# The second input projection as seven half-block products in place of eight, with weight sums formed in the first

## The chip, the cores and the metric

One NeuronCore of a Trainium2 chip runs the whole program. The metric is the device time of one execution in microseconds.

## The reference

Two decoder layers run for a prompt of 2048 tokens and for 64 sample tokens (8 sequences of 8), with D_MODEL = 1024. Layer 0 runs gated linear attention and retention side by side; layer 1 is a gated DeltaNet with a causal convolution of width 4. Each layer is

```
x <- x + gate(c) * RMSNorm_post(mixer(RMSNorm_pre(x) * (1 + scale(c)) + shift(c)))
```

What the change touches is layer 1's input projection and what follows it directly: the normed and scaled tokens h (2048 + 64 by 1024) times a weight array of 1024 by 4112. Its first 3072 columns are q, k and v, which then pass the convolution over tokens and a silu; the next 1024 are the gate z, which passes a silu; the last 16 are the write strength and decay. All inputs are float32, and results are compared with a float32 reference, so each product is formed in three passes (below).

## The kernel before, in words

The phases run one after the other: `inab` (`phase_in_ab`, L630, the first input projection, to about 603 us), `mixab` (`phase_mix_ab`, L1352, the first mixer, to about 1011), `inc` (`phase_in_c`, L1882, the second input projection, 1012.8 to 1746.7) and `mixc` (`phase_mix_c`, L2355, the second mixer).

Both projections are tiled alike. Tokens go in four blocks of 512. A group is one PSUM bank of 128x512: `product` (L620, its matmul is L625) runs over 8 k tiles of 128 and over PASSES, which are high x high, high x low and low x high, since every operand is kept as a 16-bit upper half and a 16-bit lower half. That makes 24 matmuls of 512 columns a group. PE works through the groups of a block in an order written out by hand, and ACT evacuates each bank; four banks form a ring.

`inab` has 27 groups a block. Blocks 1 and 2 run from 167 to 311 and from 311 to 455 us. ACT evacuates gate and value groups at L913 into `inab_vz`, from where SP stores them (L800); POOL forms lower halves (`split_lo`, L537) and the norm's rstd (L403, L405); DVE rotates q and k (L1030 to L1037, "r chain"), which SP stores at L784. `Prep` (L337) prepares the next block's four tiles of 128 tokens: a square sum on ACT, rstd on POOL, the norm on DVE (L410), eight transposes on PE (L417, "tile turn"), scaling on ACT and DVE (L498, L508), upper halves on ACT and lower halves on POOL. SP's waits, stores and loads stand in one fixed order for each block.

`mixab` ends with `Early` (L1258), which prepares the first 512 tokens of layer 1 beside the last of the mixer: scaling, upper and lower halves (L1319 on ACT, L1336 on DVE, L1342 on POOL). Then `Finish` (L1133) closes the sample tokens: DVE's copy L1732, two small matmuls, a pow on POOL, two DVE operations, a store (L1202). SP also loads the first weights of layer 1.

`inc` keeps all of its weights in SBUF: in block 0, ACT (L568) and POOL (L574) split them into halves while PE works. A block is 24 qkv groups, 8 z groups, one quarter group (the last 16 columns, four column strips of PE at once) and one group that turns its result. ACT moves a qkv group to `ub` (L2071), DVE runs the convolution on it (L2169 to L2175: halo copy, one multiply, three multiply-adds), ACT applies silu (L2064), SP stores it. After the last block the sample tokens follow: their own products (L2314), turns, the decay chain on ACT, and a sample convolution on DVE (L2208 to L2215). The last DMAs of the phase are issued at L2152 and L2153, and `mixc` begins with L3088.

Of the kernel before, what the change touches and what calls it, by code (L numbers as in the profile page):

```python
# [206 lines left out]
def phase_ada(nc, io, modT):  # L207

    io["modT"] = modT
    io["cT"] = nc.dram_tensor("tmp_cT", (P, KT * C9), F32, kind="Internal").ap()  # L210

# [407 lines left out]

def product(nc, dst, lhs, rhs, before=lambda k: None):  # L620
# [9 lines left out]
def phase_in_ab(nc, io, modT, seq):  # L630
# [67 lines left out]

    c_in, silu, ctr, cT_ready = ph.sem("c_in"), ph.sem("silu"), ph.sem("ctr"), ph.sem("cT_ready")
# [22 lines left out]
    unit_at = {g: [AHEAD + i for i, s in enumerate(slots) if s == g] for g in slots}  # L722

# [9 lines left out]
    def _(sp):  # L733
# [26 lines left out]

        def outputs(b, n, tiles, next_loads):
# [9 lines left out]
            next_x(0)  # L771
            sp.wait_ge(u_done, b + 1)
# [9 lines left out]
            next_x(1)  # L782
            sp.wait_ge(r_done, b + 1)
# [12 lines left out]
            for j in range(4 * tiles):  # L796
# [4 lines left out]
                             vz[:, j % 4, :]).then_inc(vz_out[j % 4], 16)  # L801
                if j == 4:
                    next_x(3)
# [5 lines left out]
        with sp.Fori(0, nb - 2) as b:  # L809
            outputs(b, BLK, TPB, [(4 * b + 6 + tc, tc % 2, P) for tc in range(4)])  # L810
            rot_load(b + 1, BLK)
        b = nb - 2
        outputs(b, BLK, TPB, [(4 * b + 6 + tc, tc % 2, (P, P, NS, 0)[tc]) for tc in range(4)])
        rot_load(b + 1, BLK)
# [10 lines left out]
        sp.wait_ge(pre_in, 64)  # L825
        for i in range(4):
            sp.wait_ge(vz_out[i], 16 + 16 * nt + (32 if i < 2 else 0))
# [3 lines left out]
    def _(pool):  # L831
# [30 lines left out]
    def _(act):  # L862
# [27 lines left out]
        def groups(b, n, next_square, first=False, rows_at={}):  # L890
            chain.turn(2 * b)

            for q, g in enumerate(order(n)):
# [50 lines left out]
                if first and g in GATES:  # L944
                    cond.gates(act, GATES[g])
                if g in rows_at:
# [7 lines left out]
        for b in range(1, nb - 1):  # L954
            groups(b, BLK, [(4 * b + 4 + tc, P) for tc in range(4)])
        rows_out.load(act, 0)
# [4 lines left out]
    def _(dve):  # L961
# [20 lines left out]

        def work(b, n, next_tiles):
# [13 lines left out]

            nx(0)

# [13 lines left out]
            nx(1)  # L1013
            dve.wait_ge(decays, b + 1)
# [13 lines left out]
            nx(2)  # L1028
            dve.wait_ge(cs_in, 16 * (b + 1))
# [2372 lines left out]
```

## Time and profile before

| | |
|---|---|
| runs | 2570.91 us median of 3 (2569.47 to 2582.24) |
| profiled execution | 2569.45 us, its span 2567.6 us |
| PE busy | 2422.2 us, 94% of the span |
| DVE, ACT, POOL busy | 1259.1, 862.2, 780.3 us |
| first input projection | to 603 us, four blocks of 144 us |
| second input projection | 1012.8 to 1746.7 us |

PE is TensorE's matmuls, PEld its weight loads (they run beside matmuls), DVE is VectorE, ACT ScalarE, POOL GpSimd, SP the engine that issues most DMAs. Busy time says how long an engine had work; whether it sets the time is read from the windows and from what ended its idle times.

### The profile page before, as it was taken

The numbers are of one execution on the slowest core, as the hardware profiler recorded it, in microseconds if no ns is written. First come the engines' busy times: TensorE is split into PE (matmuls) and PEld (weight loads), VectorE is DVE, ScalarE is ACT, GpSimd is POOL, SyncE is SP. The second block draws the span as 40 slices with busy tenths as digits, with TensorE's granted clock in tenths as the row PEclk, the third lists the DMA queues.
The fourth block names the chain that finished last, engine by engine and source line by source line (L and its number), as shares of the span: only waits on it lengthen the run. The fifth ranks groups of instructions, "written<-read, shape, count | busy, mean of one in ns | idle before, by whom it ended". The sixth has DMA issues, their size and how long they took to land. (4 is left out here: it accounts for less than half of the span.)

```text
span 2567.6 us, 52403 instructions
## 1 busy us (share of the span) xinstructions
PE 2422.2 (94%) x20691; PEld 1467.2 (57%) x20756; DVE 1259.1 (49%) x2613; ACT 862.2 (34%) x2490; POOL 780.3 (30%) x847
## 2 busy tenths in 40 slices
PE   6989999997899987999999999996899999999997
PEld 2444444444556632444444444455788888888885
DVE  3431213131687753993543626515546464554655
ACT  2633232222111113442322322225444444545431
POOL 2540000021111102551010000005656566565653
PEclk8999999998999997999999999998999999999998
DMA  8541202134544544552121112116523132222213
GB/s 297 154 146 42 99 33 91 38 119 152 203 141 155 176 165 122 155 163 84 66 71 54 62 55 80 50 43 172 141 72 105 60 106 70 84 92 81 79 32 94
DMA packets 254515, 270.00 MB, mean 105 GB/s; under 512 B 30263, under 2 KB 188023, under 8 KB 254314
## 3 DMA queue, kind: packets, MB, share of 16 engines
q1 hardware_dynamic: 186762, 219.27, 26.0%
q10 hardware_dynamic: 67552, 47.84, 6.6%
q8 instruction: 152, 2.49, 0.4%
q14 instruction: 49, 0.40, 0.0%
HBM read 179.70 MB, written 87.36 MB: 104 GB/s over the span
## 5 line engine op out<-in xcount | busy, mean ns | idle before, releaser
L625 PE MATMUL inc_b<-raw_next,inc_w_hi 128*128 128x512 f16 (+1 forms) x760 | 227.9, 381 | 3.2 <-POOL inc_w_lo L574 2.0
L625 PE MATMUL inc_b<-keep,inc_w_hi 128*128 128x512 bf16 (+1 forms) x762 | 227.2, 379 | 1.4 <-ACT inc_ub L2071 0.2
L625 PE MATMUL inab_b<-inab_wt,keep 128*128 128x512 f16 x768 | 168.3, 381 | 10.2 <-POOL inab_wt L574 10.2
L625 PE MATMUL inab_b<-inab_wt,raw_next 128*128 128x512 f16 x768 | 166.4, 379 | 0.0
L1171 PE MATMUL mixab_y<-keep,mixab_oT_hi 128*128 128x512 f16 x512 | 152.5, 379 | 7.6 <-DVE mixab_f_y L1251 5.9
L2173 DVE SCALAR_TENSOR_TENSOR inc_acc<-inc_ub,inc_taps,inc_acc 128x512 f32<-128x512 f32 x192 | 152.0, 792 | 6.8
L2071 ACT ACTIVATE inc_ub<-inc_b 128x512 f32<-128x512 f32 x96 | 56.9, 593 | 251.1 <-PE inc_b L625 247.0
L625 PE MATMUL inc_b<-raw_next,inc_w_lo 128*128 128x512 bf16 x368 | 140.1, 381 | 0.0
L625 PE MATMUL inc_b<-keep,inc_w_lo 128*128 128x512 bf16 x366 | 138.8, 379 | 0.0
L2169 DVE COPY inc_ub<-inc_halo 128x3 f32<-128x3 f32 x96 | 26.0, 271 | 228.3 <-ACT inc_ub L2071 228.3
L625 PEld LDWEIGHTS inab_b<-inab_wt,keep 128*128 128x128 bf16 (+1 forms) x768 | 75.2, 98 | 101.0 <-issue 12.7
L625 PEld LDWEIGHTS inc_b<-raw_next,inc_w_hi 128*128 128x128 f16 x768 | 75.3, 98 | 91.3 <-issue 3.0
L625 PEld LDWEIGHTS inab_b<-inab_wt,raw_next 128*128 128x128 bf16 (+1 forms) x768 | 75.1, 98 | 90.0
L625 PEld LDWEIGHTS inc_b<-keep,inc_w_hi 128*128 128x128 f16 x768 | 75.0, 98 | 89.4
L913 ACT ACTIVATE inab_vz<-inab_b 128x512 f32<-128x512 f32 x66 | 39.2, 598 | 243.6 <-PE inab_b L625 181.3
L2576 POOL TENSOR_TENSOR mixc_levels<-mixc_BT,raw_next 128x512 f32<-128x512 f32 (+1 forms) x82 | 110.2, 1374 | 1.5 <-DVE mixc_BT L2862 1.5
L410 DVE TENSOR_SCALAR keep<-keep,inab_rstd 128x1024 f32<-128x1024 f32 (+1 forms) x13 | 10.2, 788 | 204.6 <-POOL inab_rstd L405 204.4
L1171 PE MATMUL mixc_y<-mixc_w_hi,mixc_oT_hi 128*128 128x512 f16 x256 | 98.1, 383 | 6.7 <-DVE mixc_oT_lo L2954 6.7
L537 POOL TENSOR_TENSOR raw_next<-keep,raw_next 128x1024 f16<-128x1024 f32 x12 | 27.6, 2296 | 249.7 <-ACT raw_next L532 249.7
L537 POOL TENSOR_TENSOR keep<-keep 128x1024 f16<-128x1024 f32 x12 | 26.4, 2202 | 243.4 <-ACT keep L532 243.4
L1171 PE MATMUL mixc_y<-mixc_w_hi,mixc_oT_lo 128*128 128x512 f16 x256 | 97.6, 381 | 0.0
L1171 PE MATMUL mixc_y<-mixc_w_lo,mixc_oT_hi 128*128 128x512 f16 x256 | 97.6, 381 | 0.0
(590 smaller groups left out, 5954.5 us busy)
## 6 DMA issues: line engine op xcount, KB each, us to landing
tmp_qkv<-stage_next SPq DMA_DIRECT2D x98, 256.0 KB, 2.0
stage_next<-in_w_in_c ACTq DMA_DIRECT2D x30, 512.0 KB, 4.5
inab_stage<-in_w_in_ab ACTq DMA_DIRECT2D x24, 512.0 KB, 4.1
raw_next<-tmp_qkv SPq DMA_DIRECT2D x8, 1536.0 KB, 6.7
mixc_qkv<-tmp_qkv SPq DMA_DIRECT2D x8, 1536.0 KB
inab_wt<-in_w_ada SPq DMA_DIRECT2D x10, 1024.0 KB, 15.3
keep<-in_x_prompt SPq DMA_DIRECT2D x16, 512.0 KB, 4.1
tmp_v<-inab_vz SPq DMA_DIRECT2D x32, 256.0 KB, 4.0
```

What stands on the lines that cost most here:

```text
L410: dve.tensor_scalar(self.xn[0:n, :], self.x[par][0:n, :], self.rs[0:n, par:par + 1], None, ALU.mult).then_inc(self.xnd, 1)
L537: pool.tensor_tensor(room[1][:, :, col:col + n], self.hf[:, :, 0:n], room[0][:, :, col:col + n], ALU.subtract).then_inc(self.lo_done, 1)
L625: last = nc.tensor.matmul(dst, lhs(a, k), rhs(b, k), start=(k == 0 and i == 0), stop=(k == KT - 1 and i == len(PASSES) - 1))
L913: act.activation(vz[:, j % 4, :], src[:], ACT.Copy if j < (2 * TPB if n == BLK else 1) else ACT.Silu).then_inc(evac, 1)
L1171: last = self.nc.tensor.matmul(self.banks[half][0:n, :], (self.oT_hi, self.oT_lo)[a][:, h, 0:n], self.w[b][:, h, half * 512:(half + 1) * 512],
L2071: act.activation(ub[g % 2][:, CONV - 1:], src[:], ACT.Copy).then_inc(evac, 1)
L2169: chain.link(dve.tensor_copy(u_[:, 0:CONV - 1], h_))
L2173: chain.link(dve.scalar_tensor_tensor(a_v, win(i), taps[:, c, i:i + 1], a_v, ALU.mult, ALU.add))
L2576: pool.tensor_tensor(BTm[w][0:n], BT[0:n, :, 0:HB], bc(tv[f"pick{w}"][0:n].unsqueeze(1), [n, H, HB]), ALU.mult).then_inc(btm_ready, 1)
```

## The change

**Seven products for eight.** A step of `inc` is now a 2x2 block product: two channel tiles of 128 by the block's two halves of 256 tokens, with k in two halves of 512. In Winograd's form, seven products of sums of quarters replace eight, each of 4 k tiles x 3 passes = 12 matmuls of 256 columns. There are 64 steps, 16 a block: 12 "units" for q, k and v (channel tiles u and u + 4) and 4 z steps, "gate items", one after every three units. In the last block a unit step has 288 columns: 32 of the sample tokens ride along with each half. The order on PE is `begin(n)` (products 1 and 6), `finish(n-1)` (4 and 3), `rest(n)` (2, 5 and 7). Between them ACT forms the first sum and the c11 corner, DVE the second and third sum and the corners c22, c21 and c12 from PSUM; the corners go to `ub`. The convolution's first multiply is now ACT's, its halo copies are POOL's, and a `Pairs` class replaces `Prep`: it forms differences of the tokens' quarters on DVE, upper halves on ACT and lower halves on POOL (3 parts a set, 6 sets of 3584 elements a partition, one small sample set).

**Weight sums.** The seven weight factors (four of them the sums s1 to s4, three plain quarters) of all 16 unit columns are formed in blocks 1 and 2 of `inab` by `PairWeights`, in 64 steps, 32 a block. A step: SP loads four 128x128 quarters, DVE forms the sums into a spare PSUM bank, ACT the upper halves, POOL and DVE the lower halves, SP stores both to DRAM (`tmp_w7`). There is one buffer `a_out` for the plain quarters, and two of everything else. In `inc` they are streamed: a ring of two slots of 1.8 MB each (one unit's seven factors, 7 DMAs of 256 KB with rows of 2 KB), refilled by SP as soon as a product has used its factor. The z factors (4 x 1.8 MB) are loaded at the start of `inc`, ahead of the refills. The SP and DVE loops of `inab` are written out; POOL's work there stands by group.

**The end of `mixab`.** `Early` also forms differences and the 7 operands of block 0, and SP loads the ring's two slots (14 DMAs) before it stores the sample tokens.

**The sample work of `inc`** moves between the last block's steps: halo and strengths after step 3 and 4, cumulated sums after 5, turned tails and sample convolutions after 8 and 12, the sample's z product after 10; only the last third of tails and sample convolution is left for the end.

```diff
+class PairWeights:
...
+    def next(self, sp, n):
+        u, k = divmod(n, 4)
+        sp.wait_ge(self.a_lo, n + 1)
+        sp.dma_start(self.dst[u, 0:3, :, k].rearrange("m p e x -> p m e x"), self.a_out[:]).then_inc(self.a_stored, 16)
+        if n + 2 < PAIR_STEPS:
+            sp.wait_ge(self.s_done, n + 1)
+            self.load(sp, n + 2)
+        if n >= 1:
+            self.store_s(sp, n - 1)
...
+        dve.tensor_tensor(s1, a21, a22, ALU.add).then_inc(self.s1_done, 1)
+        dve.tensor_tensor(s3, a11, a21, ALU.subtract)
+        dve.wait_ge(self.s1_done, n + 1)
+        dve.tensor_tensor(s2, s1, a11, ALU.subtract).then_inc(self.s2_done, 1)
+        dve.wait_ge(self.s2_done, n + 1)
+        dve.tensor_tensor(s4, a12, s2, ALU.subtract).then_inc(self.s_done, 1)
...
+    def hi(self, act, n):
+        act.wait_ge(self.raw_in[n % 2], 32 * (n // 2 + 1))
+        wait(act, self.a_stored, 16 * n)
+        act.activation(self.a_out[:, :, 0, :], self.raw[n % 2][:, P:4 * P].rearrange("p (m x) -> p m x", m=3), ACT.Copy).then_inc(self.a_hi, 1)
+        act.wait_ge(self.s_done, n + 1)
+        wait(act, self.s_stored[n % 2], 16 * (n // 2))
+        act.activation(self.s_out[n % 2][:, :, 0, :], self.banks[n % 2][:].rearrange("p (m x) -> p m x", m=4), ACT.Copy).then_inc(self.s_hi, 1)
...
+        pool.tensor_tensor(self.a_out[:, :, 1, :], self.raw[n % 2][:, P:4 * P].rearrange("p (m x) -> p m x", m=3), self.a_out[:, :, 0, :],
+                           ALU.subtract).then_inc(self.a_lo, 1)
...
+    W7_TWICE = (16, 18, 20, 22, 24, 26, 28)
+    w7_slots = [g for g in order(BLK) for _ in range(2 if g in W7_TWICE else 1) if not 5 <= g < 7]
...
-            for tc in range(TPB):
-                prep.rstd(pool, TPB * b + TPB + tc, tc % 2, P)
-                prep.split_lo(pool, TPB * b + TPB + tc, tc * P, P, prep.at(b + 1))
+            for g in order(BLK):
+                for tc in range(TPB):
+                    if g == SQUARE[tc]:
+                        prep.rstd(pool, TPB * b + TPB + tc, tc % 2, P)
+                    if g == HI[tc]:
+                        prep.split_lo(pool, TPB * b + TPB + tc, tc * P, P, prep.at(b + 1))
+                for step in w7_at(b, g):
+                    w7.lo(pool, step)
...
+                for step in w7_at(b, g):
+                    w7.hi(act, step)
...
+    def differences(self, dve):
+        dve.wait_ge(self.m_a, 4)
+        dve.wait_ge(self.m_v, 4)
+        dve.tensor_tensor(self.tmp[2], self.b22, self.b12, ALU.subtract).then_inc(self.t3, 1)
+        dve.wait_ge(self.t3, 1)
+        dve.tensor_tensor(self.tmp[0], self.b12, self.b11, ALU.subtract).then_inc(self.t1, 1)
+        dve.wait_ge(self.t1, 1)
+        dve.tensor_tensor(self.tmp[1], self.b22, self.tmp[0], ALU.subtract).then_inc(self.t2, 1)
+        dve.wait_ge(self.t2, 1)
+        dve.tensor_tensor(self.tmp[3], self.b21, self.tmp[1], ALU.subtract).then_inc(self.t4, 1)
...
+        sp.wait_ge(fin.yp, 2 * nt + 1)
+        for u in range(2):
+            for m in FIRST_NEEDED:
+                sp.dma_start(ring_slot(io, u)[:, m].rearrange("p k e x -> p (k e x)"), io["w7"][u, m].rearrange("p k e x -> p (k e x)")
+                             ).then_inc(io["ring_in"][u][m], 16)
...
+        def refill(n, i):
+            if unit(n) is None or turn_of(n) + 2 >= QKV * nb:
+                return
+            w = turn_of(n) + 2
+            m = A_OF[i]
+            sp.wait_ge(done[i], n + 1)
+            sp.dma_start(ring[w % 2][:, m].rearrange("p k e x -> p (k e x)"), io["w7"][w % QKV, m].rearrange("p k e x -> p (k e x)")
+                         ).then_inc(ring_in[w % 2][m], 16)
...
+            for k in range(4):
+                for j, (x, y) in enumerate(PASSES):
+                    start, stop = first and k == 0 and j == 0, k == 3 and j == len(PASSES) - 1
+                    if u is not None:
+                        last = nc.tensor.matmul(bank[:, 0:w], ring[turn_of(n) % 2][:, ma, k, x, :], room.part(y, mb, k, slice(0, w)),
+                                                start=start, stop=stop, skip_group_check=not first)
+                    else:
+                        zu, tp = ORDER[n % G]
+                        last = nc.tensor.matmul(bank[:, 0:HN].rearrange("p (v x) -> p v x", v=2), room.part(x, mb, k, slice(tp * P, (tp + 1) * P)),
+                                                zw[:, 2 * zu:2 * zu + 2, ma, k, y, :], start=start, stop=stop, skip_group_check=not first)
+            last.then_inc(done[i], 1)
...
+        def finish(n):
+            pe.wait_ge(s3_ready, n + 1)
+            product7(n, 4, bank_b[n % 2], False)
+            pe.wait_ge(c22, n + 1)
+            product7(n, 3, bank_c[n % 2], False)
+        def rest(n):
+            pe.wait_ge(s1_ready, n + 1)
+            product7(n, 2, bank_a, False)
+            wait(pe, c12, n - 1)
+            product7(n, 5, bank_c[n % 2], True)
+            pe.wait_ge(s2_ready, n + 1)
+            product7(n, 7, bank_b[n % 2], False)
...
-            for g, label in enumerate(ORDER):
-                dst = bank[(b * G + g) % RING]
-                pe.wait_ge(evac, b * G + g + 1)
-                if g < NCH:
-                    need(g)
-                    last = product(nc, dst[:], lambda e, k: W[e][:, k, g * P:(g + 1) * P], lambda e, k: h[e][:, k, :])
-                elif label < NCH + 2 * TPB:
-                    i, tc = divmod(label - NCH, TPB)
-                    need((NCH + 3, NCH + 7)[i])
-                    c0 = NCH * P + i * 512
-                    last = product(nc, dst[:], lambda e, k: h[e][:, k, tc * P:(tc + 1) * P], lambda e, k: W[e][:, k, c0:c0 + 512])
-                elif label == NCH + 2 * TPB:
-                    need(NCH + 8)
-                    for step in range(2 * len(PASSES)):
...
+        for n in range(N):
+            b, p = divmod(n, G)
+            begin(n)
+            for q in tile_at(b, p, TURN, S_TURN):
+                tiles.turn(pe, q)
+            if n:
+                finish(n - 1)
+            rest(n)
+            if n == 0:
```

PE from the last matmul of `mixab` into `inc` before (`inc_t<-tab,stage_next` turns the convolution's taps, `raw_next` holds the tokens' halves, `inc_w_hi` and `inc_w_lo` the weights):

```order
L1225 MATMUL mixab_y<-mixab_f_ss,mixab_sc 128x1
L134 UNCONDITIONAL_BRANCH
L2232 UNCONDITIONAL_BRANCH
L2238 MATMUL inc_t<-tab,stage_next 128x4 x16
L2238 MATMUL inc_b<-tab,stage_next 128x4 x8
L625 MATMUL inc_b<-raw_next,inc_w_hi 128x512 x2
L625 MATMUL inc_b<-raw_next,inc_w_lo 128x512
```

And now (line numbers are those of the changed kernel; `inc_a`, `inc_b`, `inc_c` are PSUM banks, `keep` the ring of weight factors, `stage_next` the tokens' operands):

```order
L1398 MATMUL mixab_y<-mixab_f_ss,mixab_sc 128x1
L134 UNCONDITIONAL_BRANCH
L2819 UNCONDITIONAL_BRANCH
L2837 MATMUL inc_a<-stage_next,keep 128x256 x12
L2837 MATMUL inc_b<-stage_next,keep 128x256 x12
L2837 MATMUL inc_a<-stage_next,keep 128x256 x12
L2837 MATMUL inc_c<-stage_next,keep 128x256 x12
L2837 MATMUL inc_b<-stage_next,keep 128x256 x12
L2874 MATMUL inc_t<-tab,stage_next 128x4 x16
L2874 MATMUL inc_m<-tab,stage_next 128x4 x8
L2837 MATMUL inc_a<-stage_next,keep 128x256 x12
L2837 MATMUL inc_b<-stage_next,keep 128x256 x24
```

The taps no longer stand ahead of the products; five products of step 0 come first (its last two, 4 and 3, follow step 1's first two). PE now, from the third unit of block 0 to its first z step (`inc_zw` holds the z factors; there was nothing like it before):

```order
L2837 MATMUL inc_a<-stage_next,keep 128x256 x12
L2837 MATMUL inc_b<-stage_next,keep 128x256 x12
L2145 MATMUL inc_t<-tab,raw_next 128x128 x8
L2837 MATMUL inc_b<-stage_next,keep 128x256 x12
L2837 MATMUL inc_c<-stage_next,keep 128x256 x12
L2837 MATMUL inc_a<-stage_next,keep 128x256 x12
L2837 MATMUL inc_c<-stage_next,keep 128x256 x12
L2837 MATMUL inc_b<-stage_next,keep 128x256 x12
L2899 MATMUL inc_m<-inc_tab,stage_next 128x16 x4
L2841 MATMUL inc_a<-inc_zw,stage_next 128x256 x12
```

Products 4 and 3 of the step before (the second `inc_b` and the first `inc_c`) stand between products 6 and 2 of this one, and a tile's turn ahead of them.

ACT in block 1 of `inab`, groups 15 to 17, before (the waits are semaphores: `inab_mm` is a finished group, `inab_vz_out` a stored one):

```order
L913 ACTIVATE inab_vz<-inab_b 128x512 [waits inab_vz_out0,inab_mm]
L498 ACTIVATE keep<-inab_t,modT 128x128 [waits inab_h_lo,inab_x_turned]
L498 ACTIVATE keep<-inab_t,modT 128x128 x3
L376 ACTIVATE keep,inab_sumsq<-keep 128x1024 [waits inab_x_turned,inab_x_in0]
L913 ACTIVATE inab_vz<-inab_b 128x512 [waits inab_vz_out1,inab_mm]
L913 ACTIVATE inab_vz<-inab_b 128x512 [waits inab_vz_out2,inab_mm]
```

And now (`inab_a_out` is the plain quarters' buffer, `inab_stage<-inab_m` the sums' upper halves):

```order
L1064 ACTIVATE inab_vz<-inab_b 128x512 [waits inab_vz_out0,inab_mm]
L499 ACTIVATE keep<-inab_t,modT 128x128 [waits inab_h_lo,inab_x_turned]
L499 ACTIVATE keep<-inab_t,modT 128x128 x3
L377 ACTIVATE keep,inab_sumsq<-keep 128x1024 [waits inab_x_turned,inab_x_in0]
L719 ACTIVATE inab_a_out<-inab_stage 128x3x128 [waits inab_w7_a_stored,inab_w7_raw_in1]
L722 ACTIVATE inab_stage<-inab_m 128x4x128 [waits inab_w7_s_stored1,inab_w7_s]
L1064 ACTIVATE inab_vz<-inab_b 128x512 [waits inab_vz_out1,inab_mm]
L719 ACTIVATE inab_a_out<-inab_stage 128x3x128 [waits inab_w7_a_stored,inab_w7_raw_in0]
L722 ACTIVATE inab_stage<-inab_m 128x4x128 [waits inab_w7_s_stored0,inab_w7_s]
L719 ACTIVATE inab_a_out<-inab_stage 128x3x128 [waits inab_w7_a_stored,inab_w7_raw_in1]
L722 ACTIVATE inab_stage<-inab_m 128x4x128 [waits inab_w7_s_stored1,inab_w7_s]
L1064 ACTIVATE inab_vz<-inab_b 128x512 [waits inab_vz_out2,inab_mm]
```

Between two evacuations of ACT now stand one or two steps of weight sums, each with a wait for the store of the step before (`inab_w7_a_stored`).

## Rows read from the trace of the kernel before

**Rows 1.** The page of the whole span: head, then busy time of each engine.
```profile
span 2567.6 us, 52403 instructions
...
PE 2422.2 (94%) x20691; PEld 1467.2 (57%) x20756; DVE 1259.1 (49%) x2613; ACT 862.2 (34%) x2490; POOL 780.3 (30%) x847
```

**Rows 2.** Busy time by stretch; columns: stretch, length, engines, PE clock, DMA share, GB/s.
```profile
311.00:455.00 144.00, 143.34 (x691) 66.66 (x694) 29.50 (x38) 42.47 (x71) 11.45 (x12) 1.00 0.17 61
...
1012.80:1708.40 695.60, 687.19 (x3289) 320.64 (x3338) 370.89 (x653) 205.75 (x357) 116.86 (x72) 0.99 0.26 84
1708.40:1746.70 38.30, 27.41 (x290) 18.71 (x288) 15.93 (x32) 16.97 (x32) 0.07 (x2) 0.91 0.25 55
1012.80:1050.00 37.20, 35.11 (x173) 17.33 (x178) 22.02 (x26) 15.53 (x23) 20.35 (x11) 0.91 0.56 159
```

**Rows 3.** Timeline in first projection, block 2; columns: start us, us, engine, operation.
```profile
401.00 0.60 ACT L913 ACTIVATE inab_vz<-inab_b 128x512 f32<-128x512 f32 x1 [4.58 <-PE inab_b L625]
...
406.18 0.60 ACT L913 ACTIVATE inab_vz<-inab_b 128x512 f32<-128x512 f32 x1 [3.64 <-PE inab_b L625]
...
413.20 2.50 DVE L1037 TENSOR_TENSOR inab_r<-inab_r,inab_tab 128x512 f32<-128x512 f32 x4
...
415.72 0.38 SPq L784 DMA_DIRECT2D tmp_qk<-inab_r  x1
...
423.90 0.60 ACT L913 ACTIVATE inab_vz<-inab_b 128x512 f32<-128x512 f32 x1 [17.12 <-DMA tmp_v<-inab_vz]
```

**Rows 4.** Timeline, PE, the sample tokens' products of 64 columns.
```profile
599.22 0.23 PE L625 MATMUL inab_b<-inab_y,inab_wc_hi 128*128 128x64 bf16 x2
...
599.29 0.13 PEld L625 LDWEIGHTS inab_b<-inab_y,inab_wc_hi 128*128 128x128 f16 x2
...
602.00 0.19 PE L625 MATMUL inab_b<-inab_y,inab_wc_lo 128*128 128x64 bf16 x1
```

**Rows 5.** The page's groups: weight loads of the second projection.
```profile
L625 PEld LDWEIGHTS inc_b<-keep,inc_w_hi 128*128 128x128 f16 x768 | 75.0, 98 | 89.4
```

**Rows 6.** Timeline around 403 us: tile turn on PE, a lower half on POOL.
```profile
402.62 2.12 POOL L537 TENSOR_TENSOR raw_next<-keep,raw_next 128x1024 f16<-128x1024 f32 x1 [20.71 <-ACT raw_next L532]
...
406.49 1.09 PE L417 MATMUL inab_t<-tab,keep 128*128 128x128 f32 x8 [0.35 <-DVE keep L410]
```

**Rows 7.** Groups by form on DVE, 1050 to 1746 us.
```profile
L2173 DVE SCALAR_TENSOR_TENSOR inc_acc<-inc_ub,inc_taps,inc_acc 128x512 f32<-128x512 f32 x184 | 144.3, 784 | 6.6
```

**Rows 8.** Timeline at the end of the second projection.
```profile
1726.61 0.69 DVE L2208 TENSOR_TENSOR keep<-keep,inc_taps 128x512 f32<-128x512 f32 x1
...
1741.52 1.33 ACTq L2153 DMA_DIRECT2D tmp_brow_s<-inc_acc  x1
...
1746.68 1.97 PE L3088 MATMUL mixc_B<-tab,raw_next 128*128 128x128 f32 x8 [10.88 <-SPq L2466]
```

**Rows 9.** DMA queues, and issues by tile: KB each, median us to landing.
```profile
q1 hardware_dynamic: 186762, 219.27, 26.0%
q10 hardware_dynamic: 67552, 47.84, 6.6%
...
tmp_v<-inab_vz SPq DMA_DIRECT2D x32, 256.0 KB, 4.0
tmp_z<-inab_vz SPq DMA_DIRECT2D x32, 256.0 KB, 2.0
```

**Rows 10.** Timeline at the end of the first mixer.
```profile
1001.42 1.60 POOL L1342 TENSOR_TENSOR raw_next<-mixab_v,raw_next 128x512 f16<-128x512 f32 x1
...
1001.93 1.64 DVE L1336 TENSOR_TENSOR raw_next<-mixab_v,raw_next 128x512 f16<-128x512 f32 x1
...
1003.49 0.21 DVE L1732 COPY mixab_sc<-mixab_tab 128x128 f32<-128x128 f32 x1
...
1006.76 1.11 SPq L1202 DMA_DIRECT2D tmp_x_s<-mixab_f_x  x2
...
1012.81 0.37 PE L2238 MATMUL inc_t<-tab,stage_next 4*128 4x4 f32 x2 [8.47 <-SPq L1956]
```

More of the change, by code:

```diff
@@ L759, in _, with w7_next @@
         sp.sem_inc(r_free, 1)
+        def w7_next(b, *gs_):
+            for g in gs_:
+                for step in w7_at(b, g):
+                    w7.next(sp, step)
         def outputs(b, n, tiles, next_loads):
@@ new lines, in _ @@
+        for n in range(N + 1):
+            b, p = divmod(n, G)
+            if n < N and unit(n) is not None:
+                set_halo(n, 0)
+            if n >= 1 and unit(n - 1) is not None:
+                save_halo(n - 1, 0)
+            if n < N and unit(n) is not None:
+                set_halo(n, 1)
+            if n >= 1 and unit(n - 1) is not None:
+                save_halo(n - 1, 1)
+            if n < N:
+                for q in tile_at(b, p, SQUARE, S_SQUARE):
+                    tiles.rstd(pool, q)
+                for c, part in lower_parts(b, p):
+                    tiles.lower(pool, c, part)
+            if b == LAST and p in J_DONE:
+                tail_rows(J_DONE[p])
@@ new lines, in tap, with silu @@
+        def tap(n, side):
+            w, g = turn_of(n), channels(unit(n))[side]
+            for sem in ((c21, c22), (c11, c12))[side]:
+                act.wait_ge(sem, n + 1)
+            wait(act, acc_out[n % 2], 32 * (n // 2))
+            act.activation(acc[n % 2][:, side, :], ub[w % 2][side][:, CONV - 1:], ACT.Copy, scale=taps[:, g, CONV - 1:CONV]).then_inc(tapped[side], 1)
+        def silu(n, side):
+            act.wait_ge(conv_done[side], turn_of(n) + 1)
+            act.activation(acc[n % 2][:, side, :], acc[n % 2][:, side, :], ACT.Silu).then_inc(silu_done[side], 1)
@@ new lines, in conv @@
+        def conv(n, side):
+            w, g = turn_of(n), channels(unit(n))[side]
+            u_, a_v = ub[w % 2][side], acc[n % 2][:, side, :]
+            dve.wait_ge(tapped[side], w + 1)
+            dve.wait_ge(halo_set[side], w + 1)
+            for i in range(CONV - 1):
+                ins = dve.scalar_tensor_tensor(a_v, u_[:, i:i + BLK], taps[:, g, i:i + 1], a_v, ALU.mult, ALU.add)
+                if i < CONV - 2:
+                    chain.link(ins)
+            ins.then_inc(conv_done[side], 1)
@@ L2232, in _ @@
+        sample_conv(2)
     @block.tensor
     def _(pe):
[L2234 to L2247 removed]
@@ new lines, in quarters @@
+        def quarters(b):
+            room = rooms[b % 2]
+            wait(pe, ab_ready, b)
+            if b == 0:
+                pe.wait_ge(taps_ready, 1)
+                pe.wait_ge(wab_lo, 1)
+            for j, terms in enumerate((((0, 0), (4, 4)), ((0, 0), (0, 12), (4, 8)))):
+                for step in range(len(terms) * len(PASSES)):
+                    (kw, kh), (x, y) = terms[step // len(PASSES)], PASSES[step % len(PASSES)]
+                    for q in range(4):
+                        last = nc.tensor.matmul(misc[q * 32:(q + 1) * 32, j * HN:(j + 1) * HN], wab[:, kw + q, x, :],
+                                                (room.hi, room.lo)[y][:, kh + q, 0:HN], start=j == 0 and step == 0,
+                                                stop=step == len(terms) * len(PASSES) - 1, skip_group_check=True)
+            last.then_inc(abq_mm, 1)
```

1187 lines of the change are left out of this document (777 added, 410 removed).

## The prediction

> **What bounds the kernel now.** I read the page first. TensorE is busy for 94% of a span of 2567.6 us; VectorE, the next, for 49% [rows 1]. The windows then show the two stages that the change touches. A middle block of the first input projection, 311 to 455, keeps PE busy for 143.3 of 144 us at full clock (2.4 GHz), with ACT at 42.5, DVE at 29.5, POOL at 11.5 and the DMA engines at 0.17. The second projection from 1012.8 to 1708.4 has PE at 687.2 of 695.6, DVE at 370.9, ACT at 205.8, POOL at 116.9, DMA at 0.26 [rows 2]. So PE alone sets both, and the rest has room. Behind the second projection lie 38.3 us of sample work and tails, PE busy for 27.4 of them [rows 2].
>
> What a matmul costs decides the change. Two PSUM evacuations of consecutive groups start at 401.00 and 406.18; 24 matmuls of 512 columns lie between: 215.8 ns each [rows 3]. At 64 columns, 96 matmuls start from 599.22 to 602.00, 29.3 ns each, and every one has its own 128x128 weight load [rows 4]. The line through both is 2.7 ns + 0.416 ns per column, so **256 columns: 109.2 ns**. Both levels show no price for the load, which has 98 ns of its own at 512 columns [rows 5] and must lie under 109 now. It is the nearest thing to a catch, and a rival below.
>
> **The second projection.** Before: 4 blocks x 32 groups x 24 x 215.8 = 662.9 us of products in the 733.9 us from 1012.8 to 1746.7. Now: 4 x 16 steps x 7 products x 12 = 5376 matmuls x 109.2 = 587.1 us. Other PE work: 13 tile turns and 3 tail turns of 8 transposes, 1.09 each [rows 6], 17.4; 32 sample columns more in the last block's 12 x 84 = 1008 matmuls x 32 x 0.416 = 13.4; the sample gates, 48 pairs of 64x256, about 5.2; the quarter groups, which use four column strips at once, 4 x 15 x 109.2 = 6.6; taps, halo, cumulated sums and token columns about 6. That makes 48.6, and 635.7 in all. The last two products and the last turn, 3.7, lie in the tail and are priced there: 632.0.
>
> The tail after them: third sum, corners and last conv on DVE 4.3 (256-column operations at half of 0.78, three of 0.78 [rows 7]); seven 128x512 operations at 0.69 of the last sample conv [rows 8] 4.8; silu and tails on ACT 1.9; five DMA issues 2.0; and from the last issue's end (1742.85) to mixc's first matmul (1746.68) 3.8 as now [rows 8]: 17.
>
> Stalls of PE that I add, 30: the third step waits for a refill queued on SP behind the z weights (4 x 896 = 3584 rows of 2 KB; from bytes, packets and share, q1 takes 57 ns for a packet of 1174 B and q10 40 ns for one of 708 B [rows 9], so about 89 ns here, over 16 engines 20 us, with tiles of x and the refills' own rows 28, while PE is there after 20) about 8; quarter evacuation 4; sample decay chain and sample convs on DVE ahead of its second sum 7; tile preparation ahead of DVE's and ACT's sums 4; clock at the start (0.91 in 1012.8 to 1050 [rows 2]) 2; DVE held by POOL's halves 5. The last is read from one place: at 1001.93 a 128x512 subtraction of two SBUF operands on DVE takes 1.64, and ends 0.55 after POOL's, where such an operation alone takes 0.69 [rows 8, 10]. The Trainium skill agrees ("GPSIMD Engine Reference", section 1, Specifications: GpSimd's SBUF interfaces are shared with VectorE, which contends when it has two SBUF inputs).
>
> Per step DVE has five half-width sums (0.4 each) and six conv operations (4.7): 6.7 of the 84 x 109.2 = 9.2 us that PE needs; ACT two silus, two taps, two moves: 3. Both are hidden in a plain step; conv's first operations and half of the halo copies left DVE. A unit's weights are 896 rows, 896 x 89 ns / 16 = 5.0 us of all engines, and a slot is asked again two unit steps, 18 us, later; each matrix is refilled as soon as its product is done. The DMA share rises from 0.26 by about 0.33. PE and the 18 us hide it: I cost it at nothing. If that cover goes, because SP stands at another wait and the refills behind it come late, 2 us a unit step are 92. Sum: 632.0 + 17 + 30 = 679 against 733.9: **-55** (bounds -85 with no stalls, +37 with starved refills).
>
> **The end of the first mixer.** Early now forms block 0's operands, 7168 elements a partition with an upper and a lower half where it was 4096. On DVE these are four differences of 1024 and four lower halves of 1024, where four of 512 stood, and DVE has to pass them to reach the copy at 1003.49 that the end's chain hangs on (sample mean, pow, two sums, store at 1006.76, first operation of the next phase at 1012.81 [rows 10]). Eight at twice 0.69 are 11, and more where POOL takes its turn (1.60 and 1.64 side by side); the four old ones, 5, go away; ACT's wait for them was short. I take 9 and not 6, since 14 weight loads now stand on SP ahead of the sample store. **+9** (0 if the gates' wait covers it, 15 if each takes 1.64 x 2).
>
> **The first projection, blocks 1 and 2.** 32 steps of sums in each of two 144-us blocks: ACT 2 more operations (0.45 and 0.60, by 0.60 for 512 columns [rows 3]), DVE five (about 2.2, by 0.69 for 512 [rows 8]), POOL one (0.8, by 2.12 for 128x1024 [rows 6]). Per block ACT gets to 42.5 + 34, DVE to 29.5 + 70, POOL to 11.5 + 26 [rows 2]: room for all. What counts is the order. There is **one** a_out: ACT's copy of step n waits until SP has stored step n-1, and SP issues that store only after POOL's half. So a step can't be shorter than copy 0.45, POOL 0.8, store about 2.0 (256 KB stores of z land in 2.0, of v in 4.0 [rows 9]), three hand-overs of 0.1: 3.55; I take 3.8, since SP issues four DMAs a step at 0.38 each [rows 3]. PE has two groups, 10.36 us, per three steps in the later half of the block, so 3.45 a step: short by 6 x (3 x 3.8 - 10.36) = 6 us a block, since ACT must come round to evacuate and only four banks lie between; and about 2 where the order begins. The vz stores wait in the same SP queue: before, ACT already sat idle for 17.12 until v's store let it go on at 423.90, because SP first had to wait for DVE's r work up to 415.7; it had banks in hand, and PE went on [rows 3]. Now POOL's rstd for that block no longer stands behind a lower half, so the r work ends 10 us earlier, but five steps' stores stand on SP between. At the start of block 3 ACT waits for the last sums before it loads rows: 3 to 5. In all 2 x 8 + 4 = **+20** (8 at 3.45 a step; 38 at 4.3). The sums' DMAs, 64 x (384 + 512 + 512) = 90,112 rows of 512 B at about 33 ns / 16, are 186 us of all engines spread over 288, on a share of 0.17 to 0.25: not full, but their landings lengthen; that is why I am above 3.55.
>
> **The sum.** The profiled execution took 2569.45, the median of the runs 2570.91, so it stands for them. 2569.5 - 55 + 9 + 20 = **2544**; own range 2520 to 2575. Below 0.5% (13 us) a measurement of this kernel can't be told from no change.
>
> **Rivals.** (B) *The sums keep pace.* Stores land in 2.0 and the step takes 3.45; the second projection stalls for half of 30. For it: ACT and DVE have room; against: v's stores take 4.0. 2569.5 - 70 + 5 + 8 = 2512. Chance 0.18.
> (C) *Slower: the single a_out.* If a store of 384 rows among these lands in 4.0, as v's do [rows 9], a step is 5.6; 32 steps then need 179 us against 144, and ACT, which evacuates for PE, stands in the copy's wait. By the same sum, 2 + 6 x (3 x 5.6 - 10.36) = 41 a block, 86 in all in place of 20: 2609. It decides from a step of 4.5 on (42), where the gain is spent but for a few us. Chance 0.13.
> (D) *POOL's lower halves reach PE.* Six sets of 3584 elements a partition at 2.12 per 1024 [rows 6] take 7.4 each, 45 in all; if DVE can do none of its sums meanwhile, PE loses 45 and not 5: 2584. For it: the 1.64; against: DVE has 2.5 us of slack a step, and the sums read PSUM. Chance 0.10.
> (E) *The load does not hide.* If a load of 128x128 ran only behind the matmul before, a 256-column matmul would be 109 + 98 [rows 5] = 207 ns, and 5376 x 98 = 527 come on top: 3060. The 29.3 ns of rows 4 hold a full load each and leave no room for it. Chance 0.02. The Trainium skill speaks for this one ("TensorE: Matmul & The Clock Gate", Part 3: Packing small matmuls, The mechanism: a load overlaps only when it goes to another row group); the rows differ from it, and the rows decide.
>
> **How the numbers follow.** The forecast and what lies between it and B and C has 0.57. Of it some 0.42 is faster than 2557; with B that is 0.60. C, E and the upper ends of D and of the forecast with starved refills are slower than 2583: 0.21. The rest, 0.19, is within 0.5%. The range leaves out what of B lies below 2500 (no stall at all) and most of C: 2500 to 2592.
>
> **What would show it.** Right: in the second projection steps of 9.2 to 9.5 us with PE over 95% busy, 256-column matmuls about 109 ns apart, a stage of about 680 us; in blocks 1 and 2 of the first projection lengths of 150 to 155 us, with ACT's idle time before its 128x384 copy ended by the a_out store. Wrong: PE waiting for ring loads at step after step; a block 1 of over 165 us; or no idle before that copy, which makes B true.

## The result and the profile after

The changed kernel takes 2620.36 us (median of 4 runs, 2615.59 to 2623.04) against 2570.68 before: ratio **1.0181, 95% interval 1.0148 to 1.0214**. It is slower, where the forecast was 2544 and the range ended at 2592. The profiled execution has a span of 2613.8 us, 46.2 more than before. The page:

```profile
span 2613.8 us, 58705 instructions
...
PE 2371.3 (91%) x23067; PEld 1693.5 (65%) x23084; DVE 1416.1 (54%) x3034; ACT 968.0 (37%) x2726; POOL 872.4 (33%) x1092
```

PE has 51 us less to do than in rows 1, and the span is longer all the same. The stages tell where it went. The stretches below run between marks at the same instructions in both traces: the first matmul of the quarter group in each block of the first input projection (L1096 before, L1269 now), the first of `inc`, the first of `mixc`.

| stretch | before | after | change |
|---|---|---|---|
| to block 0's mark | 55.8 | 55.2 | -0.6 |
| first projection, block 0 | 151.5 | 154.7 | +3.2 |
| block 1 | 131.6 | 177.7 | **+46.1** |
| block 2 | 131.6 | 181.8 | **+50.2** |
| block 3 | 128.4 | 134.7 | +6.3 |
| sample tokens and `mixab` | 413.9 | 421.0 | +7.1 |
| `inc`, from its first matmul | 733.9 | 668.0 | **-65.9** |
| `mixc` | 820.9 | 820.8 | 0 |

(A middle block takes 131.6 us by these marks, and block 1 begins at 207.3; the 144 us, and the 167, 311 and 455 in the text ahead, were bounds of windows and not of blocks.) The second projection gained more than forecast, and the first lost it all. Its windows, by block (columns as in rows 2):

```profile
209.80:387.50 177.70, 139.69 (x633) 63.09 (x636) 76.41 (x183) 68.25 (x122) 39.67 (x41) 0.91 0.56 165
387.50:569.40 181.90, 139.52 (x633) 62.85 (x637) 82.47 (x198) 71.69 (x129) 43.35 (x46) 0.91 0.59 172
569.40:704.10 134.70, 130.53 (x614) 58.72 (x622) 32.61 (x51) 38.58 (x55) 22.21 (x14) 0.97 0.33 104
```

DMA share rose from 0.17 in rows 2 to 0.56 and 0.59, DVE to 76 to 82 us a block, ACT to 70: none is near full. In block 1 PE is busy for 139.7 us on the same 633 matmuls that took 130.9 before, at a mean granted clock of 0.91 against 1.00 (the full 2.4 GHz), and idle for 38. What PE waited for, block 1 and then block 2 (columns: engine, waiting line, what released it, us in total, times, longest):

```profile
PE inab_b L742 <- ACT inab_vz L1064: 21.1, 5, 13.1
PE inab_t L418 <- DVE keep L411: 8.4, 2, 7.5
```

```profile
PE inab_b L742 <- ACT inab_vz L1064: 23.8, 6, 13.1
PE inab_t L418 <- DVE keep L411: 8.9, 2, 7.8
PE inab_b L1269 <- POOL keep L538: 8.3, 1, 8.3
PE inab_b L1269 <- POOL raw_next L538: 8.1, 1, 8.1
```

In both blocks ACT comes late to an evacuation, once by 13.1 us; a tile turn waits for DVE's norm, and the first matmuls after blocks 1 and 2 wait 8 us each for the last lower half on POOL (the row of 8.3 is the one at the end of block 1). ACT itself waited, in block 1:

```profile
ACT inab_a_out L719 <- DMA tmp_w<-inab_a_out: 53.4, 17, 18.0
ACT inab_stage L722 <- DMA tmp_w<-inab_stage: 30.6, 23, 1.8
ACT inab_stage L722 <- DVE inab_m L707: 18.6, 5, 6.5
```

Here is the long one, in block 1 (timeline; start, length, engine):

```profile
287.03 2.28 DVE L1197 TENSOR_TENSOR inab_r<-inab_r,inab_cs 128x2048 f32<-128x2048 f32 x1
...
293.88 2.50 DVE L1204 TENSOR_TENSOR inab_r<-inab_r,inab_tab 128x512 f32<-128x512 f32 x4
...
296.40 0.38 SPq L921 DMA_DIRECT2D tmp_qk<-inab_r  x1
...
300.67 0.35 SPq L369 DMA_DIRECT2D keep<-in_x_prompt  x1
301.06 0.43 SPq L937 DMA_DIRECT2D tmp_v<-inab_vz  x1
301.54 0.43 SPq L682 DMA_DIRECT2D tmp_w<-inab_a_out  x1
...
306.28 0.52 ACT L719 ACTIVATE inab_a_out<-inab_stage 128x384 f16<-128x384 f32 x1 [18.04 <-DMA tmp_w<-inab_a_out]
...
307.81 0.60 ACT L722 ACTIVATE inab_stage<-inab_m 128x512 f16<-128x512 f32 x1 [1.00 <-DMA tmp_w<-inab_stage]
...
309.95 0.52 ACT L719 ACTIVATE inab_a_out<-inab_stage 128x384 f16<-128x384 f32 x1 [1.55 <-DMA tmp_w<-inab_a_out]
...
312.57 0.59 ACT L1064 ACTIVATE inab_vz<-inab_b 128x512 f32<-128x512 f32 x1
...
313.22 13.40 PE L742 MATMUL inab_b<-inab_wt,raw_next 128*128 128x512 f16 x48 [13.14 <-ACT inab_vz L1064]
```

To be read from the end: PE stood for 13.14 us until ACT's evacuation at 312.57. ACT had sat 18.04 us until the store of the step before had landed, at 306.28. POOL had its lower half ready at 285.0, but SP issued that store at 301.54 only, since in its fixed order it first waits for the end of DVE's rotation (296.4), stores its result, waits for that to land, and stores a value tile. The landing took 4.7 us of the wait, twice the median of 2.1 us of these stores in the two blocks. Then ACT has two steps in a row to do, each with waits (306.28 to 312.57), and evacuates behind them.

### The profile page after: what moved, and what is told of

Read it like the earlier page. It is cut to its first block and busy times, and to the rows that moved or that the text cites. A ratio compares the mean times of both kernels' runs of the same rounds, so it can differ in the third digit from the quotient of the medians.

```text
span 2613.8 us, 58705 instructions
## 1 busy us (share of the span) xinstructions
PE 2371.3 (91%) x23067; PEld 1693.5 (65%) x23084; DVE 1416.1 (54%) x3034; ACT 968.0 (37%) x2726; POOL 872.4 (33%) x1092
## 5 line engine op out<-in xcount | busy, mean ns | idle before, releaser
L2728 DVE SCALAR_TENSOR_TENSOR inc_acc<-inc_ub,inc_taps,inc_acc 128x512 f32<-128x512 f32 x288 | 243.7, 846 | 9.2 <-ACT inc_acc L2571 2.4
L2507 POOL COPY inc_halo<-inc_ub 128x3 f32<-128x3 f32 x96 | 50.2, 525 | 363.6 <-DVE inc_ub L2716 224.1
L726 POOL TENSOR_TENSOR inab_a_out<-inab_stage,inab_a_out 128x384 f16<-128x384 f32 x64 | 61.3, 958 | 226.9 <-ACT inab_a_out L719 226.9
L2837 PE MATMUL inc_b<-inc_room,keep 128*128 128x256 bf16 (+3 forms) x864 | 109.9, 279 | 2.4 <-DVE stage_next L2698 2.4
L2571 ACT ACTIVATE inc_acc<-inc_ub,inc_taps 128x512 f32<-128x512 f32 x96 | 68.7, 722 | 107.5 <-DVE inc_ub L2716 68.9
L2837 PE MATMUL inc_b<-stage_next,keep 128*128 128x256 bf16 (+1 forms) x864 | 106.2, 275 | 0.7 <-DVE stage_next L2698 0.7
L2575 ACT ACTIVATE inc_acc<-inc_acc 128x512 f32<-128x512 f32 x96 | 60.4, 629 | 120.3 <-DVE inc_acc L2728 120.3
L1344 PE MATMUL mixab_y<-keep,mixab_oT_lo 128*128 128x512 f16 x256 | 97.0, 379 | 0.0
L2837 PEld LDWEIGHTS inc_b<-inc_room,keep 128*128 128x128 f16 x864 | 84.4, 98 | 18.1 <-DVE stage_next L2698 2.7
L2837 PEld LDWEIGHTS inc_b<-stage_next,keep 128*128 128x128 f16 x864 | 85.3, 99 | 11.5 <-DVE stage_next L2698 1.0
```

Source lines behind the costliest of these rows:

```text
L726: pool.tensor_tensor(self.a_out[:, :, 1, :], self.raw[n % 2][:, P:4 * P].rearrange("p (m x) -> p m x", m=3), self.a_out[:, :, 0, :], ALU.s ...
L1344: last = self.nc.tensor.matmul(self.banks[half][0:n, :], (self.oT_hi, self.oT_lo)[a][:, h, 0:n], self.w[b][:, h, half * 512:(half + 1) * 512],
L2507: pool.tensor_copy(halo[:, g, :], ub[w % 2][side][:, BLK:]).then_inc(halo_saved[side], 1)
L2571: act.activation(acc[n % 2][:, side, :], ub[w % 2][side][:, CONV - 1:], ACT.Copy, scale=taps[:, g, CONV - 1:CONV]).then_inc(tapped[side], 1)
L2575: act.activation(acc[n % 2][:, side, :], acc[n % 2][:, side, :], ACT.Silu).then_inc(silu_done[side], 1)
L2728: ins = dve.scalar_tensor_tensor(a_v, u_[:, i:i + BLK], taps[:, g, i:i + 1], a_v, ALU.mult, ALU.add)
```

## Experiments

All are compared with the kernel before on the same chip (2577 to 2578 us there, and not 2571), so one experiment is set beside another by its ratio. "Blocks" are the lengths of blocks 0 to 3 by the marks above.

**1. The stores alone.** Engine work and loads for the sums are done for the first step only; both stores of each step stay in SP's order.

```diff
+        if n:
+            return
         act.wait_ge(self.raw_in[n % 2], 32 * (n // 2 + 1))
```

> Leaves out: the weight sums of all steps but the first, and the loads for them; the two stores of each of the 64 steps stay on SP in their places and always write the first step's halves, so the second projection multiplies by the same weights throughout (its instructions and transfers are unchanged). Theory H (the hand-overs of a step, ACT to POOL to SP to ACT and SP's queue, cost the 105 us between the first matmul of block 1 and of the sample tokens in the first projection): that stretch, 494.3 us now against 391.6 before, falls to 392 to 400, and the program takes 2515 to 2525. Theory T (the traffic of the stores itself slows what PE needs): the stretch stays above 420.

Measured 2511.55 us, ratio 0.9747 (0.9713 to 0.9782), blocks 152.6, 131.0, 131.0, 128.4. Its windows of blocks 1 and 2:

```profile
209.80:340.80 131.00, 131.00 (x637) 61.14 (x636) 33.03 (x43) 41.09 (x67) 14.02 (x13) 1.00 0.58 180
340.80:471.90 131.10, 131.10 (x641) 61.15 (x642) 31.44 (x38) 40.10 (x65) 13.12 (x12) 1.00 0.57 175
```

PE never stops at three times the DMA share of before, and the stretch from block 1's mark takes 390.5 us (392 to 400 expected; the program, too, is somewhat below its range). The stores' traffic costs nothing, which rules out theory T, and without the steps the change is 2.5% faster than the kernel before. That fits theory H. It does not show H alone, since the loads and the steps' engine work are gone with the hand-overs; experiment 7, which has all of them, settles that. Which hand-over it is stays open here.

**2. A second a_out.**

```diff
-        wait(act, self.a_stored, 16 * n)
+        wait(act, self.a_stored[n % 2], 16 * (n // 2))
```

> Everything as in the change, with a second buffer for the plain quarters' halves (the sample tokens' tables are loaded again after it). Theory A (the single buffer alone, rival C of the prediction): a step is no longer bound by copy, lower half and landing in a row; each of blocks 1 and 2 gives back most of its 46 to 50 us, the program takes 2530 to 2550. Theory Q (the waits of 18 us, and the 13 us that PE loses in each of the two blocks, come from SP and DVE standing at the rotation of q and k): one more step is let through, the 13 us shrink to some 8, and the program takes 2580 to 2605.

Measured 2604.96 us, ratio 1.0110 (1.0081 to 1.0139), blocks 153.6, 172.1, 178.3, 134.9. Theory A alone falls: the single buffer by itself is worth 0.7%, and the program is at the upper end of Q's range. ACT's long wait does not go, it moves to the next instruction, the copy of the sums. In block 1:

```profile
ACT inab_stage L724 <- DMA tmp_w<-inab_stage: 72.2, 19, 20.0
```

Q is not borne out in full either: PE's longest wait was to shrink from 13 us to some 8 and is 13.4.

**3. The rotation's stores later.** SP stores rotated q and k after the fifth value store, DVE forms the sums of groups 16 to 18 between the rotation's operations.

```diff
-            sp.wait_ge(r_done, b + 1)
...
                 if j == 4:
+                    r_stores()
                     next_x(3)
+                if j == 7:
+                    sp.wait_ge(out, 80 * b + 80)
+                    sp.sem_inc(r_free, 1)
```

> One buffer as in the change; SP stores the rotated q and k after the fifth value store instead of ahead of all of them, and DVE forms the sums of groups 16 to 18 between the operations of the rotation. Theory Q: the 18 us wait and PE's 13 us go in both blocks, with the slow clock behind them: 2575 to 2590. Theory A: the wait moves only, the step's own 4.2 us remains the bound: 2605 to 2618.

Measured 2583.05 us, ratio 1.0017 (1.0001 to 1.0032), blocks 142.6, 165.4, 172.3, 135.0. In Q's range, but with luck: 11 to 12 us of the gain are in block 0, which forms no sums (142.6 for 153.6 in experiment 2 and 154.7 in the change; experiment 8), and Q had not counted them; without them the time would be some 2595, above the range. The longest wait of PE for an evacuation is 5.5 us now, as Q says, but the clock stays at 0.93 and 0.90 in the two blocks, tile turns and POOL's lower halves are waited for as before (17 and 14 us over both), and the blocks still are 34 and 41 too long.

**4. Both, and the double steps spread.**

```diff
-    W7_TWICE = (16, 18, 20, 22, 24, 26, 28)
+    W7_TWICE = (1, 3, 9, 16, 19, 24, 27)
```

> Both edits, and the seven double steps of a block spread over all of it (groups 1, 3, 9, 16, 19, 24, 27) instead of the later half. If Q and A together hold all of the loss: 2515 to 2530, faster than the kernel before. If the tile turns and the lower halves of the next block's tiles wait for a further cause (POOL or DVE full of sums' work): 2540 to 2570.

Measured 2568.23 us, ratio 0.9953 (0.9937 to 0.9969), blocks 143.8, 163.3, 167.8, 130.2. So a further cause exists. It is not a full engine (DVE 86 us of 163). ACT's waits in block 1 name it:

```profile
ACT inab_stage L724 <- DMA tmp_w<-inab_stage: 54.3, 19, 8.2
ACT inab_stage L724 <- DVE inab_m L707: 32.2, 9, 6.5
```

ACT no longer waits for a store of a_out, but for the sums of the very step it is at (DVE forms them in the same slot), and for the store of the sums two steps ago. Hence theory L. What the spread of the double steps does by itself was not run.

**5. Sums one slot later.** ACT takes the upper halves of step n's plain quarters and of step n-1's sums, DVE the sums ahead of the older lower halves.

```diff
-                    w7.hi(act, step)
+                    w7.hi_a(act, step)
+                    if step:
+                        w7.hi_s(act, step - 1)
```

> The change with one edit: in each slot ACT forms the plain quarters' upper halves of step n and the sums' upper halves of step n-1, and DVE the sums of step n ahead of the lower halves of step n-1, so that ACT never waits for the sums that DVE forms in the same slot. One a_out and SP's order stay. Theory L (what holds ACT in the runs with both edits, 54 us for stores of sums and 32 us for DVE's sums in block 1, is that it takes each step's sums in the step's own slot): a gain of its own, 2590 to 2608. Theory Q: with SP at the rotation's stores the 18 us wait stays, and the time stays within 2608 to 2620.

Measured 2591.60 us, ratio 1.0062 (1.0042 to 1.0082), blocks 154.6, 164.4, 170.7, 133.0. L has a gain of its own, 1.2%.

**6. That and experiment 3**, one a_out:

> That edit and the later stores of the rotated q and k, with one a_out and the double steps in the later half. Q and L together: blocks 1 and 2 fall from 165 and 172 to 140 to 150 us each, the program to 2535 to 2555. If the single a_out is still a bound (4.2 us a step against 3.45): 2560 to 2575.

Measured 2558.45 us, ratio 0.9933 (0.9914 to 0.9953), blocks 143.3, 152.7, 161.5, 131.5. The program lies between the two ranges, and the blocks are longer than the 140 to 150 that Q and L alone would leave them. Over both blocks, ACT's waits for the sums are gone, and one row stands for nearly everything:

```profile
ACT inab_a_out L719 <- DMA tmp_w<-inab_a_out: 165.6, 54, 13.1
```

3.1 us for each of 54 steps: what still holds ACT is the single a_out, and experiment 7 takes that away.

**7. All three** (2, 3 and 5; double steps where the change has them):

> The same with two a_out, double steps in the later half as in the change. If Q, L and A hold all: blocks 1 and 2 at 132 to 136 us, the program 2505 to 2520, 2 to 3% faster than the kernel before. If transfers or DVE's rotation still hold a step now and then: 2520 to 2545.

Measured 2507.90 us, ratio **0.9738 (0.9722 to 0.9755)**, blocks 142.4, 133.2, 135.1, 130.2. Its windows of blocks 1 and 2, and ACT's waits over both (`inab_tab` is the second buffer):

```profile
197.20:330.50 133.30, 131.18 (x641) 61.13 (x644) 85.56 (x182) 67.67 (x121) 46.54 (x41) 1.00 0.73 215
330.50:465.50 135.00, 131.15 (x636) 61.11 (x636) 89.68 (x198) 72.13 (x129) 50.36 (x45) 1.00 0.80 232
```

```profile
ACT inab_a_out L721 <- DMA inab_stage<-in_w_in_c: 48.3, 22, 6.2
ACT inab_tab L721 <- DMA inab_stage<-in_w_in_c: 36.1, 21, 5.1
ACT inab_stage L726 <- DVE inab_m L707: 18.4, 8, 3.8
ACT inab_stage L726 <- DMA tmp_w<-inab_stage: 13.5, 37, 1.9
```

In both ranges that were set. The steps issue all that they did, loads and transfers to a share of 0.80 included, and PE is busy 131.2 of 133.3 us at clock 1.00, so neither the loads nor the engines' work had cost the time. ACT still waits for over 100 us, for loads above all, and PE waited for an evacuation once in both blocks, for 1.7 us.

**8. The kernel before, with the later stores alone** (SP's part of experiment 3):

> The kernel before, with SP storing the rotated q and k after the fifth value store. The run of the change with that edit (and DVE's sums between the rotation) had a block 0 of 142.6 us against 152 to 155 in all others; if SP's order alone does it, block 0 falls from 151.5 to 142 to 144 here too and the program is 8 to 10 us faster, 2560 to 2570 beside 2570 to 2578; if not, no change.

Measured 2567.30 us, ratio 0.9956 (0.9943 to 0.9969), blocks 142.7, 131.6, 131.6, 128.4. The same order on SP had cost the kernel before 9 us in block 0, where ACT has weights to split behind an evacuation that waits. PE's wait there for POOL's half of the split weights (L574) falls from 10.2 to 1.7 us. The evacuation in the trace of the kernel before:

```profile
154.56 0.60 ACT L913 ACTIVATE inab_vz<-inab_b 128x512 f32<-128x512 f32 x1 [14.17 <-DMA tmp_v<-inab_vz]
```

**9. Experiment 7 without the later stores** (and without DVE's sums between the rotation's operations, which came with them in experiment 3):

> The change with two a_out and each step's sums taken one slot later, but with SP storing the rotated q and k where the change has it, ahead of the value stores. Theory Q+L+A (three hand-overs, each of which holds blocks 1 and 2 once the others are gone): blocks 1 and 2 at 145 to 160 us with the long ACT wait still behind the rotation, block 0 at 152 to 155, the program 2530 to 2565. If the slack of two buffers and a slot covers SP's stand at the rotation: 2515 to 2525, which is the 2508 of the run with all three and the 10 us of block 0.

Measured 2533.43 us, ratio 0.9823 (0.9802 to 0.9845), blocks 154.5, 139.4, 144.1, 128.7. The program is in the first range, blocks 1 and 2 are shorter than its 145 to 160. Of the 25 us beside experiment 7, 12 are block 0 and 13 are what SP's stand at the rotation still costs (with DVE's sums behind it: the two parts of this edit were not run apart in blocks 1 and 2). PE's waits from block 1's mark on:

```profile
PE inab_b L746 <- ACT inab_vz L1074: 15.5, 4, 8.4
PE inab_b L1283 <- POOL keep L538: 1.5, 1, 1.5
```

**10. Experiment 7, with the z factors loaded during steps 1 and 3 of `inc`.**

```diff
+            if n in (1, 3):
+                z_load(n - 1)
+                z_load(n)
```

> The run with all three edits (2508), and in the second projection the four z loads are issued during steps 1 and 3 instead of ahead of all refills. The 7.3 us that PE waits at step 2 for a ring load should go: 2499 to 2504. If the z factors then come late for step 3 or the wait moves to another load: 2506 to 2512.

Measured 2503.51 us, ratio **0.9704 (0.9686 to 0.9722)**, the fastest here and 2.96% under the kernel before. The number is in the first range, the mechanism is the second's: the 7.3 us at step 2 are gone from the profile, but a wait of about that size stands at the start of step 4 (steps counted from 0):

```profile
1068.45 2.74 PE L2870 MATMUL inc_a<-stage_next,keep 128*128 128x256 bf16 x12 [6.45 <-ACT inc_acc L2588]
```

ACT's corner of the z step (step 3) waits there for an output buffer. Its store, issued at 1055.1 behind two z loads, landed 12.8 us later. The profiled execution is the slowest of the four (2511). The gain over experiment 7 is at the edge of the intervals, and where it comes from is not shown.

The three hand-overs together, as ratios to the kernel before (A second a_out, Q later stores, L one slot later):

| none | A | Q | L | A, Q, spread | Q, L | A, L | A, Q, L |
|---|---|---|---|---|---|---|---|
| 1.0181 | 1.0110 | 1.0017 | 1.0062 | 0.9953 | 0.9933 | 0.9823 | 0.9738 |

A is worth 0.7% while the others stand, 2.4% on top of L and 1.95% on top of Q and L; L 1.2% alone and 2.9% on top of A (the 2.2% between "A, Q, spread" and "A, Q, L" hold the spread's removal too, and A with Q alone was not run). So A and L hide behind each other. Q does not hide: it is worth 1.6% alone, 1.3% on top of L and 0.9% on top of both, and about 0.5% of it is block 0. Differences of two ratios are good to some 0.25 to 0.45%.

## Why the prediction was wrong, step by step

**The matmul price: right.** Three groups of 12 matmuls of one block of `inc`:

```profile
1203.44 1.47 PE L2837 MATMUL inc_c<-stage_next,keep 128*128 128x256 bf16 x12
1204.76 1.47 PE L2837 MATMUL inc_b<-stage_next,keep 128*128 128x256 bf16 x12
1206.07 1.47 PE L2841 MATMUL inc_a<-inc_zw,stage_next 128*128 128x256 f16 x12
```

They start 1.31 us apart, 109 ns a matmul, the value on the line through rows 3 and 4. Rival E (loads that do not hide) is out: every one has its 128x128 load (its 3060 should have been 3071, 2544 + 527). The rule of the Trainium skill that the prediction set beside it ("TensorE: Matmul & The Clock Gate", Part 3: Packing small matmuls, The mechanism: a load overlaps only when it goes to another row group) does not hold for these rows.

**The second projection: mechanism right, stalls too large.** It gained 65.9 us where 55 were forecast. The whole stage (with the first 4 us of `mixc`):

```profile
1125.00:1797.00 672.00, 645.04 (x5968) 562.36 (x5968) 430.23 (x786) 264.20 (x517) 144.83 (x262) 0.98 0.65 205
```

and what PE waited for in it:

```profile
PE inc_a L2837 <- DMA keep<-tmp_w: 7.0, 1, 7.0
...
PE inc_b L2837 <- DVE stage_next L2698: 3.1, 2, 2.4
PE inc_b L2841 <- DVE stage_next L2698: 2.7, 4, 0.7
PE inc_m L2899 <- ACT stage_next L2597: 2.6, 3, 0.9
```

The wait of the third step for its refill was put at 8 and is 7.0; DVE's sums, with POOL's halves (rival D), were put at 7 + 5 and cost 5.8; the quarter evacuations 2.6 for 4. With 0.3 for ACT's first sum these are 15.7 of the 30 forecast. The tail, from the end of the last step's product 7 (1777.9) to `mixc` (1793.0), is 15.2 for 17. PE's own work was put too low: it is busy for 637.5 us up to 1777.7, at a mean clock of 0.99, where 632 were summed up. Refills at nothing: right, at a DMA share of 0.65.

**The end of the first mixer: right**, +7.1 for +9 (the sample tokens' stretch of the first projection is in the 7.1). The chain is as forecast, the copy L1929 stands behind Early's operations:

```profile
1103.80 1.23 DVE L1503 TENSOR_TENSOR stage_next<-raw_next 128x1024 f32<-128x1024 f32 x1
...
1104.49 4.45 POOL L1524 TENSOR_TENSOR stage_next<-raw_next,stage_next 128x2048 f16<-128x2048 f32 x1 [15.39 <-ACT stage_next L1514]
...
1105.06 4.96 DVE L1505 TENSOR_TENSOR stage_next<-raw_next,stage_next 128x1024 f32<-128x1024 f32 x1
...
1117.55 0.21 DVE L1929 COPY mixab_sc<-mixab_tab 128x128 f32<-128x128 f32 x1
...
1125.02 0.34 SPq L177 DMA_DIRECT2D inc_tab<-in_table  x1
```

**The first projection: wrong, +103 for +20.** The 20 were for blocks 1 and 2 and the start of block 3, which took 46.1, 50.2 and 6.3 more; block 0 added 3.2. This one term missed by more than the whole forecast did (83 us and 76). Here the step failed that turned a step's turn time into PE's time. It had three parts.

- *"I take 3.8"* for a step. The copies at 309.95 and 331.86 in block 1 (six of them, with five steps between) are 4.4 us apart on average. Little off, but the sum's own formula gives +42 at that value, and it was the smaller part. (Rival C sets 42 beside a step of 4.5; the formula gives 46 there.)
- *"It had banks in hand, and PE went on."* The 17.12 us wait of ACT [rows 3] was read as harmless since no engine waited for it. It used up most of the slack of four banks: 17.1 us is 3.3 groups of 5.2. In the change there is more on both sides of it. ACT had already waited 6.4 us for the same buffer (until 278.13), and the two steps from 306.28 to 312.57 stand behind the long wait: of PE's 13.1 us, 6.3 are these two steps and 6.9 lie before. I had counted that SP's later stores queue behind the rotation, and drew no price from it; and the rotation, which was to end 10 us earlier, was stored 87 and 95 us behind the marks of blocks 1 and 2 (296.4, 482.7), where it had been 77 behind both before. Experiment 3 shows the price, experiment 8 that part of it was there before.
- *Nothing at all* was put for ACT waiting inside a slot for DVE's sums and for the sums' store. The listing of the order shows that wait (`inab_w7_s_stored`, `inab_w7_s` in each second row of ACT), and it was passed over. Experiments 4 and 5 show it (1.2% alone), and experiment 9 beside 2 (2.9% on top of A).

And the stalls cost more than their length. In block 1 they are 38 us, but PE also took 8.8 us longer for the same matmuls, with a clock of 0.91; in experiment 7, where PE hardly stops, it is 1.00 again. The 38 us hold 8 for tile turns and 8 for POOL's lower half at the block's end. These fall to nothing and to one wait of 2.1 us in experiment 7, so they hang on the same hand-overs; by what path was not traced.

The prediction's own sign of being wrong, "a block 1 of over 165 us", came: 177.7. Rival C named the single a_out, gave 2609, and had 0.13. That its time was near is luck. It wanted landings of 4.0 us, and the median is 2.1; and experiment 2 takes the buffer's cause away and 2605 are left: the buffer is one of three hand-overs. Its point of decision, a step of 4.5, was set by the same formula, which knew of one wait only. Rival B (2512) gives nearly the time of experiment 7 (2508), but for another kernel, with the three hand-overs changed; for the change as it stood its condition, that the sums keep pace, was not met.

## What to carry to other kernels

Work laid "between" on an engine that evacuates PSUM is priced by its waits, not by its busy time: list every semaphore that the new instructions wait for, ask for each who signals it and what that queue stands at then, and let the engine take results one slot after they are due. A long wait that costs nothing in the trace of before is slack that is already spent; count it as such. Where several waits cover each other, taking one away can show little (0.7% for the second buffer), and only with the others gone does it show what it is worth (2.0 to 2.4%).

## What was not expected of the hardware

- A subtraction of 128x1024 on DVE took 4.96 us beside one on POOL and 1.23 just before it (both rows above): it ends 1.1 us after POOL's 4.45 us operation does. In rows 10 the same held at 1.64 and 0.69. By these rows it waits for nearly the whole of POOL's operation. Only two of the eight operations that Early now has on DVE met one on POOL (4.96 and 3.03 us); the other six took 1.21 to 1.23 each, so the stretch grew by 7.1 only.
- DMA engines at a mean share of 0.80 (experiment 7, block 2), in packets of 512 B for the most part, did not slow PE: 131.15 us busy for 636 matmuls, against 131.10 for 641 at 0.57 in experiment 1. Landings lengthened with the share: 192 KB stores took 2.1 us (median) at 0.57 in the change and 3.0 at 0.77 in experiment 7. In experiment 10, behind 3.6 MB of z loads that kept the engines full (397 GB/s from 1052 to 1058), one store of 256 KB took 12.8 us.
